# A decoder layer on eight cores: the MLP's first step ahead of the last mixer product, the last step in column halves, loads in program order

## The chip, the cores and the metric

The kernel runs on 8 cores of one Trainium2 chip. Each core does the same program on its own sequence (2048 prompt columns, 16 meta columns and 64 sample columns) with the whole set of weights; the cores don't talk to each other. The metric is the device time in microseconds of the slowest core.

## What is computed

```python
def layer(x, s_pool, s_conv, p0, ...):
    hn = rmsnorm(x, norm1_g)
    proj = hn @ w_in                                   # (B, T, 2048) = u | B | C | h
    ya, new_pool = pool_mixer(u, s_pool, p0, pool_w, pool_scale)   # causal means over 2, 4, 8, 16 rows, minus u, then 4 blocks of 128x128
    yb, new_conv = conv_mixer(bg, cg, hc, s_conv, conv_w)          # B * conv3(C * h)
    x = x + concat(ya, yb) @ w_out
    hn = rmsnorm(x, norm2_g)
    x = x + relu(hn @ w1) ** 2 @ w2                    # 1024 -> 4096 -> 1024
    return x, new_pool, new_conv
```

The layer runs once, on prompt and on sample tokens; a last rmsnorm gives y. The pooling and conv states of both are outputs too.

## The kernel before, in words

**Layout.** Features lie on the partitions, tokens in the columns. The core's 2128 columns are cut into five groups of 464, 464, 464, 448 and 288 columns (group 4 is 224 prompt and 64 sample columns). x of all groups stays in SBUF in fp32 (X1), the normed input in bf16 (H2). All else is cut from one SBUF tensor, "big", in which later buffers lie over earlier ones: w1's halves over w_in, the second w2 block over w_out, the first w2 block (W2B[0]) over UB, UBS and part of ZB, the first MLP result (A2[0]) over the rest of ZB, ZBS and PT, the second (A2[1]) and the relu tiles RB over MD and what follows.

**PSUM.** Eight banks in four pairs. Three pairs go round for all products (ps_pair), the fourth holds the two statistics banks (st_bank).

**Mixer, per group g, W(g).** A norm (Norm.whole: four squares on ScalarE, three additions of 2n columns to ACC (L520), a fold (L525), a split into a bf16 high part (L531) and a low part (L532), two ones-matmuls for the column sum (L540), Ln and Exp on ScalarE (L482, L485), eight applications (L554)). Then 32 matmuls (L626) for each of the four quarters of w_in: u, C, h, B. u is evicted to UB (u_done, L661 in groups 0 and 1, L664 later), pool_adds makes the window sums in PT (L604, L595, ScalarE's L613, L615) into MD; the last 16 columns of UB are copied to its head for the next group by GpSimd (L681). C is evicted to ZB, h multiplied in (L704), conv makes three-tap sums in CV (L718, L721, in groups 0 and 1 L727), with two columns copied to the next group's head by VectorE (L731), and b_done multiplies by B into MD (L738). There is one CV for two chunks. MD has two copies, for even and odd groups. In groups 0 and 1 the norm's factor is applied at the evictions (RSD). fold() puts pool_w into w_out (ScalarE's L786 on the pool weights, matmuls L793, evictions L796). O(g) is 64 matmuls with w_out and four adds to X (L782).

**MLP.** Twenty steps, four blocks of 1024 hidden features by five groups. w1_step is 64 matmuls, four relus on ScalarE into RB (L891) and four squares on VectorE into A2 (L894); w2_step is 64 matmuls and four adds to X (L782). In the last block each group is normed and stored as its w2_step ends (stores L587). w2_tail does the last w2_step in two halves of 144 columns, with adds L933 and the sum of squares by fp32 ones-matmuls (L548, two recorded instructions each).

**What sets the order.** Program order is written out (L860 to L875, L944 to L959):

```python
    O(0); W(2); O(1); W(3); O(2); W(4); state_out(); load_w1(0)
    O(3); O(4); load_w2(0); load_w1(1); load_w2(1); norm2(0).whole(); norm2(1).whole()
    w1_step(0)
    for si in range(ns):
        ...                       # norm2(si + 2), w1_step(si + 1), then w2_step(si) or w2_tail
```

TensorE runs its units in this order, but for the statistics matmuls, which float. All other queues are ordered by a planner (plan, L123): it simulates the program with assumed costs (VectorE 120 + 1.1 ns a column, ScalarE 150 + 0.87, GpSimd 150 + 2.2) and load times, gives each operation a due time from TensorE's schedule, and picks on each queue the ready operation that is due first; some operations may go to either of two engines. The resulting order is fixed in the program. The loads of w_in, w_out, w1, w2 and of x0 and x1 are issued by GpSimd; the other x, the pool weights (behind w_in's third quarter), the states and all stores by SyncE.

## Time and profile before

| | |
|---|---|
| time, 3 runs | 689.78 us median (689.34 to 690.92) |
| the profiled execution | 687.86 us |
| its slowest core's span (core 2) | 686.0 us |
| spans of the 8 cores | 682.2 to 686.0 us |
| mean granted TensorE clock of the cores | 0.986 to 0.992 |
| chain that ended last | PE 81%, DMA 11%, DVE 3%, issue 2% |
| read from and written to HBM | 55.69 MB, 9.24 MB |

PE is TensorE's matmuls, PEld its weight loads, DVE VectorE, ACT ScalarE, POOL GpSimd, SP SyncE. A row of the timeline has start, duration, engine, line, operation, out<-in, count and in brackets the idle time of the engine before it and what ended it. A row of a stretch has its bounds, its length, the busy time of PE, PEld, DVE, ACT and POOL, the granted clock (1.00 is full speed), the DMA share and GB/s. A row of a group has count, busy time and mean ns, idle time before it. The profile covers the slowest core; 1.9 us lie between its span and the execution's time.

### The profile page before, as it was taken

Reading aid. Unit: us, or ns where it says so; the run is one execution under the profiler, and the core shown is the slowest. Engines: PE = TensorE matmul, PEld = TensorE weight load, DVE = VectorE, ACT = ScalarE, POOL = GpSimd, SP = SyncE. Lnnn points to the kernel's source line nnn. Section 1 sums busy time; section 2 is a strip of 40 time slices with the busy share of each in tenths; the row PEclk is TensorE's granted clock in tenths of the full one; section 3 lists DMA queues with packets and bytes.
Section 4 is the critical chain, followed back from the end, with each engine's and each line's share of the span. In section 5 each row is a group of like instructions: output and inputs, shape, how many; then the busy total and the mean of one; then the engine's idle time right before and its main releaser. Section 6 shows DMA issues by size and latency. Waiting matters only on the chain.

```text
span 686.0 us, 9801 instructions; the slowest of 8 cores (682.2 to 686.0 us)
## 1 busy us (share of the span) xinstructions
PE 657.7 (96%) x3725; PEld 362.4 (53%) x3726; DVE 392.0 (57%) x542; ACT 185.7 (27%) x265; POOL 45.3 (7%) x71
## 2 busy tenths in 40 slices
PE   7969799999999999999999999999999999999993
PEld 4434354555764455565654556555556565555673
DVE  2768989789895963333333333333333333677676
ACT  3613544351615320111112101220121012433341
POOL 6411002011201000000000000000000000000000
PEclk9999999999999999999999999999999999999996
DMA  8997320000797910043340007061000000022025
GB/s 162 230 183 173 111 70 0 1 1 1 95 157 95 153 29 0 1 60 64 49 75 1 1 1 114 10 97 27 1 0 1 1 1 1 1 108 84 33 107 177
DMA packets 13598, 42.49 MB, mean 62 GB/s; under 512 B 3312, under 2 KB 7408, under 8 KB 10864
## 3 DMA queue, kind: packets, MB, share of 16 engines
q0 software_dynamic: 4672, 26.87, 23.9%
q1 hardware_dynamic: 8880, 15.00, 6.7%
q8 instruction: 30, 0.49, 0.3%
q14 instruction: 16, 0.13, 0.1%
HBM read 55.69 MB, written 9.24 MB: 95 GB/s over the span
## 4 chain that ended last, share of the span: by engine, by line
PE 81%; DMA 11%; DVE 3%; issue 2%; POOL 1%; ACT 1%; DVEq 0%; SPq 0%; ACTq 0%; POOLq 0%
PE psall L626 79%; DMA ncs<-big 5%; DMA big<-win 4%; DMA big<-pwt 2%; DVE big L554 1%; POOL big L436 1%; PE psall L548 1%; POOL big L442 1%; PE psall L540 1%; DVE big L704 1%; DVE big L520 0%; DVE big L738 0%; DVE big L721 0%; DVE big L532 0%; PE psall L793 0%
## 5 line engine op out<-in xcount | busy, mean ns | idle before, releaser
L626 PE MATMUL psall<-big 128*128 128x464 bf16 (+3 forms) x3552 | 627.7, 339 | 8.6 <-DVE big L661 5.4
L626 PEld LDWEIGHTS psall<-big 128*128 128x128 bf16 x3552 | 343.1, 98 | 291.6 <-issue 14.3
L894 DVE TENSOR_TENSOR big<-big 128x896 bf16<-128x896 f32 (+2 forms) x80 | 83.0, 1038 | 132.9 <-ACT big L891 126.7
L782 DVE TENSOR_TENSOR big<-psall,big 128x896 f32<-128x896 f32 (+2 forms) x96 | 100.5, 1048 | 100.5 <-PE psall L626 100.2
L891 ACT ACTIVATE big<-psall 128x896 f32<-128x896 f32 (+2 forms) x80 | 69.9, 874 | 289.3 <-PE psall L626 288.9
L510 ACT ACTIVATE big<-big 128x928 f32<-128x928 f32 (+3 forms) x64 | 54.9, 863 | 81.2 <-DVE big L782 37.9
L554 DVE SCALAR_TENSOR_TENSOR big<-big,psall 128x464 bf16<-128x464 f32 (+5 forms) x112 | 62.5, 611 | 4.8 <-ACT psall L485 4.7
L520 DVE TENSOR_TENSOR big<-big 128x928 f32<-128x928 f32 (+2 forms) x39 | 41.0, 1050 | 12.9 <-ACT big L510 12.6
L721 DVE SCALAR_TENSOR_TENSOR big<-big 128x448 f32<-128x448 f32 (+3 forms) x48 | 26.6, 602 | 1.6 <-ACT big L718 1.5
L604 DVE TENSOR_TENSOR big<-big 128x448 f32<-128x448 f32 (+24 forms) x47 | 25.6, 545 | 2.1 <-ACT big L664 0.9
L718 ACT ACTIVATE big<-big 128x448 f32<-128x448 f32 (+3 forms) x24 | 13.1, 582 | 29.6 <-DVE big L738 12.8
L548 PE MATMUL psall<-big 128*128 128x144 f32 (+1 forms) x48 | 14.0, 442 | 5.3 <-DVE big L554 3.6
L664 ACT COPY big<-psall 128x928 f32<-128x928 f32 (+3 forms) x16 | 10.1, 660 | 27.8 <-PE psall L626 27.7
L803 POOL DMA_DIRECT2D big<-w x8 | 4.4, 546 | 163.5 <-PE psall L626 163.5
L681 POOL COPY big<-big 128x16 f32<-128x16 f32 x16 | 10.7, 670 | 62.7 <-ACT big L613 41.8
L613 ACT ACTIVATE big<-big 128x448 f32<-128x448 f32 (+3 forms) x18 | 8.9, 494 | 20.1 <-DVE big L604 20.0
L548 PEld LDWEIGHTS psall<-big 128*128 128x128 f32 x48 | 8.7, 235 | 9.1 <-issue 8.9
L661 DVE TENSOR_TENSOR big<-psall,big 128x928 f32<-128x928 f32 x8 | 8.9, 1120 | 6.4 <-PE psall L626 6.4
L482 ACT ACTIVATE big<-psall 128x464 f32<-128x464 f32 (+3 forms) x16 | 8.0, 498 | 14.8 <-PE psall L540 11.1
L531 ACT CAST big<-big 128x464 bf16<-128x464 f32 (+2 forms) x13 | 7.1, 546 | 16.8 <-POOL big L525 9.1
L615 DVE TENSOR_TENSOR big<-big 128x448 bf16<-128x448 f32 (+3 forms) x13 | 6.7, 513 | 8.2 <-ACT big L613 8.2
L704 DVE TENSOR_TENSOR big<-psall,big 128x928 f32<-128x928 f32 (+2 forms) x10 | 10.1, 1014 | 2.0 <-PE psall L626 1.8
(40 smaller groups left out, 126.4 us busy)
## 6 DMA issues: line engine op xcount, KB each, us to landing
big<-w POOLq DMA_DIRECT2D x16, 1024.0 KB, 14.6
big<-x POOLq DMA_DIRECT2D x8, 464.0 KB, 13.1
y<-big SPq DMA_DIRECT2D x8, 464.0 KB, 2.5
y<-big SPq DMA_DIRECT2D x8, 448.0 KB, 2.7
big<-win POOLq DMA_DIRECT2D x6, 512.0 KB, 27.1
big<-wout POOLq DMA_DIRECT2D x2, 1024.0 KB, 46.5
big<-x SPq DMA_DIRECT2D x1, 1856.0 KB, 17.4
big<-x SPq DMA_DIRECT2D x1, 1792.0 KB, 8.6
```

What stands on the lines that cost most here:

```text
L510: fns = {"scalar": lambda e: e.activation(out=dst, in_=src, func=AF.Square), "vector": mul, "gpsimd": mul}
L520: P.add(self.adders, lambda e: e.tensor_tensor(out=ACC[:, :, 0:n], in0=ACC[:, :, 0:n], in1=SQ[si][:, :, 0:n], op=ALU.add), reads=[("ACC",) ...
L548: P.add("tensor", lambda e, i=i, t=t: e.matmul(out=PSP[3][:, b, 0:n], lhsT=ONES32, rhs=t, start=first and i == 0, stop=last and i == len(s ...
L554: P.add(eng, lambda e: e.scalar_tensor_tensor(out=self.dst(k, k + 1), in0=self.src(k, k + 1), scalar=self.gcol[:, k:k + 1], in1=PSP[3][:, ...
L604: P.add(("vector", "gpsimd"), lambda e, dstb=dstb, cur_src=cur_src, a0=lo, step=step: e.tensor_tensor(out=dstb[:, a0:L], in0=cur_src[:, a0 ...
L626: P.add("tensor", lambda e, k=k, i=i: e.matmul(out=PSP[b][:, t, 0:n], lhsT=lhs(k), rhs=rhs(k), start=(i == 0), stop=(i == len(ks) - 1)), r ...
L704: P.add("vector", lambda e: e.tensor_tensor(out=z, in0=PSP[b][:, :, 0:n], in1=y, op=ALU.mult), reads=pk(b) + ky, writes=zkeys(g, p), w=2 * ...
L718: P.add("scalar", lambda e, z=z, cv=cv, zo=zo, n=n: e.activation(out=cv, in_=z[:, zo:zo + n], func=AF.Copy, scale=cw[:, 0, c:c + 1]), read ...
L721: P.add(CONV_ENG, lambda e, z=z, cv=cv, a=zo + j * s, n=n, j=j: e.scalar_tensor_tensor(out=cv, in0=z[:, a:a + n], scalar=cw[:, j, c:c + 1] ...
L782: P.add("vector", lambda e: e.tensor_tensor(out=x, in0=PSP[b][:, :, 0:n], in1=x, op=ALU.add), reads=pk(b) + ks, writes=ks, w=2 * n, psum=True)
L891: P.add("scalar", lambda e, bk=bk, ri=ri: e.activation(out=RB[ri][:, :, 0:n], in_=PSP[bk][:, :, 0:n], func=AF.Relu), reads=pk(bk), writes= ...
L894: P.add("vector", lambda e, ri=ri, p=p: e.tensor_tensor(out=A2[ai][:, 2 * p:2 * p + 2, 0:n], in0=RB[ri][:, :, 0:n], in1=RB[ri][:, :, 0:n], ...
```

## The change

The planner: GpSimd's loads are issued in program order (so x0's and x1's pieces, which stand ahead in the program, are not passed by w_in's). An operation on GpSimd that uses the shared SBUF port waits in the plan for VectorE's more urgent ones. A floating statistic is placed by the time of all its operands.

```diff
+        loads = self.queued.get("gpsimd", [])
+        for op, then in zip(loads, loads[1:]):
+            op.order = then
+            then.need += 1
...
-            return port["gpsimd" if q == "vector" else "vector"]
+            if q == "vector":
+                return port["gpsimd"]
+            urgent = [o for o in pools["vector"] if o.port and o.due < op.due and o is not op and o.ready <= max(op.ready, free[q])]
+            return max(port["vector"], free["vector"] + sum(o.cost for o in urgent) if urgent else 0.0)
...
-                    if all(o.need == 0 or o.deps[-1].unit == f for o in us) and us[0].need == 0:
-                        at = max(free["tensor"], us[0].ready + lag)
+                    outer = [d for o in us for d in o.deps if not (d.eng == "tensor" and d.unit == f)]
+                    if all(d.done is not None for d in outer):
+                        at = max([free["tensor"]] + [d.done + (0.0 if d.eng == "tensor" else LATENCY["tensor"]) + lag for d in outer])
```

The buffers: group 1's u goes to U1; the second pair of conv chunks has a CV of its own (over UBS, so the pool state is loaded only in W(4)); the last group has a CV of four chunks; RB lies over MD[1] and A2[1] over MD[0]. The copies to the next group's head go to ScalarE. The square sums of whole norms may be added by VectorE or GpSimd, and the MLP's squares may be made by VectorE or ScalarE.

```diff
+    CVL = carve(4 * M_OUT[NG - 1] * 4, F32, "p (t n) -> p t n", t=4, at=CV_OFF)
+    CV2 = carve(2 * NB * 4, F32, "p (t n) -> p t n", t=2, at=UBS_OFF)
...
-    CT = carve(4 * NB * 4, F32, "p (c n) -> p c n", c=4, at=X_OFF[3])
+    CT = carve(4 * NB * 4, F32, "p (c n) -> p c n", c=4, at=H2_OFF[2])
+    U1 = carve(4 * (16 + PROMPT_COLS[1]) * 4, F32, "p (c n) -> p c n", c=4, at=X_OFF[3])
...
-    A2_OFF = [R2 + 16384, MD_OFF + 8 * NB * 2]
+    A2_OFF = [R2 + 16384, MD_OFF]
...
-    RB = [carve(2 * NB * 4, F32, "p (t n) -> p t n", t=2, at=MD_OFF + i * 2 * NB * 4) for i in range(2)]
+    RB = [carve(2 * NB * 4, F32, "p (t n) -> p t n", t=2, at=MD_OFF + 8 * NB * 2 + i * 2 * NB * 4) for i in range(2)]
...
-            self.adders = ("vector",)
+            self.adders = ("vector", "gpsimd")
...
+    def ubuf(g):
+        return (U1, "U1") if g == 1 else (UB, "UB")
...
-                P.add("gpsimd", lambda e, c=c: e.tensor_copy(out=UB[:, c, 0:H], in_=UB[:, c, L - H:L]),
-                      reads=[("UB", c, "new")], writes=[halo("UB", c)], w=60)
+        if g + 1 < NG and kn == ku:
+            P.add("scalar", lambda e: e.copy(out=un[:, c0:c0 + 2, 0:H], in_=u[:, c0:c0 + 2, L - H:L]),
+                  reads=[(ku, c, "new") for c in (c0, c0 + 1)], writes=[halo(kn, c) for c in (c0, c0 + 1)], w=60)
...
-            P.add("vector", lambda e: e.tensor_copy(out=ZB[:, c, H - 2:H], in_=ZB[:, c, L - 2:L]),
+            P.add("scalar", lambda e: e.copy(out=ZB[:, c, H - 2:H], in_=ZB[:, c, L - 2:L]),
```

The order, and the end:

```diff
-    O(0)
-    W(2)
-    O(1)
-    W(3)
...
+    for act in ("O0", "O1", "W2", "W3", "O2", "W4", "O3", "N0", "A0", "O4", "N1", "A1"):
...
+            if n == NG - 1:
+                state_out()
+                load_w1(0)
+                load_w2(0)
+                load_w1(1)
...
+    load_w2(1)
+    for si in range(ns - 2):
...
+        w2_step(si)
+        if 2 <= si + 2 < ns - 1:
+            w1_step(si + 2)
...
+    w2_step(ns - 2)
+    for half in range(2):
+        tail_w1(half)
+    for half in range(2):
+        tail_w2(half)
```

A0 and A1 are w1_step(0) and w1_step(1), N0 and N1 the second norms of groups 0 and 1. tail_w1(half) is the last w1_step on 144 of the 288 columns. tail_w2(half) is the last w2_step on them, with two PSUM pairs in turn (the "pt" counter), and the sum of squares first added up over the pairs 0 to 2 and then taken by four fp32 ones-matmuls instead of eight, into a bank of the third product pair that belongs to this half:

```diff
+            if p == 0:
+                f.square(p, acc[:, :, 0:m], ("TACC",))
+            else:
+                f.square(p, SQ[p % 2][:, :, 0:m], ("SQ", p % 2))
+            if p in (1, 2):
+                P.add(("vector", "gpsimd"), ... acc += SQ[p % 2] ...)
+        kst = ("ps", 2, half)
+        for i, (t, kt) in enumerate(((acc, ("TACC",)), (SQ[1], ("SQ", 1)))):
+            P.new_unit(True)
+            for h in range(2):
+                P.add("tensor", lambda e, ...: e.matmul(out=PSP[2][:, half, 0:m], lhsT=ONES32, rhs=t[:, h, 0:m], start=i + h == 0, stop=i + h == 2),
```

## Rows read from the trace of the kernel before

**Rows 1.** The page: busy time of the engines (us, share, instructions)

```profile
PE 657.7 (96%) x3725; PEld 362.4 (53%) x3726; DVE 392.0 (57%) x542; ACT 185.7 (27%) x265; POOL 45.3 (7%) x71
```

**Rows 2.** Busy time of each engine in three stretches; PEclk is the granted clock

```profile
0.00:80.00 80.00, 64.89 (x333) 32.61 (x335) 52.08 (x84) 31.77 (x47) 23.27 (x35) 0.98 0.84 184
180.00:240.00 60.00, 58.59 (x344) 33.24 (x342) 50.49 (x85) 22.16 (x36) 5.19 (x10) 1.00 0.93 132
...
670.00:686.00 16.00, 4.98 (x27) 4.37 (x24) 9.19 (x25) 1.47 (x4) 0.00 (x0) 0.61 0.55 189
```

**Rows 3.** TensorE in order of time, 12 to 80 us: start, duration, what, [idle before]

```profile
16.21 0.55 PE L626 MATMUL psall<-big 128*128 128x464 bf16 x2 [1.79 <-ACT big L561]
...
30.52 2.31 PE L626 MATMUL psall<-big 128*128 128x464 bf16 x11 [0.64 <-DVE big L525]
...
37.16 3.29 PE L626 MATMUL psall<-big 128*128 128x464 bf16 x16 [2.96 <-DVE big L661]
42.87 21.88 PE L626 MATMUL psall<-big 128*128 128x464 bf16 x112 [2.41 <-DVE big L661]
...
71.76 0.81 PE L793 MATMUL psall<-big 128*128 128x512 bf16 x3 [3.47 <-DVE big L731]
```

**Rows 4.** The stretch behind the last of these waits; 0.50 is the granted clock

```profile
73.00:76.00 3.00, 3.00 (x8) 1.08 (x9) 2.90 (x6) 3.00 (x5) 0.00 (x0) 0.50 0.73 225
```

**Rows 5.** The other engines in order of time, 24 to 54 us

```profile
26.58 4.45 POOL L681 COPY big<-big 128x16 f32<-128x16 f32 x2
...
40.57 2.16 DVE L661 TENSOR_TENSOR big<-psall,big 128x928 f32<-128x928 f32 x2 [0.52 <-PE psall L626]
...
51.45 1.28 ACT L786 ACTIVATE big<-big 128x128 bf16<-128x128 f32 x4 [7.20 <-DMA big<-pwt]
...
53.31 0.64 DVE L615 TENSOR_TENSOR big<-big 128x464 bf16<-128x464 f32 x1 [5.23 <-ACT big L613]
```

**Rows 6.** The DMA view: issues, KB each, median us from issue to landing

```profile
big<-pwt SPq DMA_DIRECT2D x1, 256.0 KB, 13.1
big<-sc SPq DMA_DIRECT2D x1, 64.0 KB, 2.3
ncs<-big SPq DMA_DIRECT2D x1, 64.0 KB, 31.4
```

**Rows 7.** TensorE and the GpSimd queue in order of time, 170 to 240 us

```profile
230.52 0.35 PE L540 MATMUL psall<-big 128*128 128x448 bf16 x1 [0.80 <-DVE big L532]
...
186.37 0.57 POOL L803 DMA_DIRECT2D big<-w  x1 [1.06 <-PE psall L626]
...
214.54 2.22 POOL L809 DMA_DIRECT2D big<-w  x4 [18.48 <-DMA ncp<-big]
```

**Rows 8.** The end in order of time, 660 to 686 us

```profile
669.16 4.81 DVE L554 SCALAR_TENSOR_TENSOR big<-big,psall 128x448 f32<-128x448 f32 x8
...
673.89 0.82 DVE L933 TENSOR_TENSOR big<-psall,big 128x288 f32<-128x288 f32 x2
...
674.23 4.30 PE L548 MATMUL psall<-big 128*128 128x144 f32 x16 [3.55 <-DVE big L554]
...
675.68 0.44 ACT L510 ACTIVATE big<-big 128x288 f32<-128x288 f32 x1 [5.72 <-PE psall L548]
...
679.41 2.29 DVE L554 SCALAR_TENSOR_TENSOR big<-big,psall 128x144 f32<-128x144 f32 x8 [2.50 <-ACT psall L485]
```

**Rows 9.** Matmuls of 640 to 686 us by shape: busy us, mean ns

```profile
L626 PE MATMUL psall<-big 128*128 128x144 bf16 x128 | 8.7, 226 | 0.0
L626 PE MATMUL psall<-big 128*128 128x288 bf16 x54 | 6.9, 286 | 0.0
```

**Rows 10.** The page and the groups of instructions over the whole span

```profile
L520 DVE TENSOR_TENSOR big<-big 128x928 f32<-128x928 f32 (+2 forms) x39 | 41.0, 1050 | 12.9 <-ACT big L510 12.6
...
L540 PE MATMUL psall<-big 128*128 128x464 bf16 (+2 forms) x26 | 7.3, 345 | 1.7 <-DVE big L532 1.6
...
L615 POOL TENSOR_TENSOR big<-big 128x448 bf16<-128x448 f32 (+2 forms) x5 | 6.2, 1238 | 14.9 <-DVE big L560 11.9 <-ACT big L613 2.2 <-DVE big L721 0.8
```

More of the change, by code:

```diff
@@ L50, in __init__ @@
         self.dma_counts = {}
+        self.queued = {}
         self.unit = 0
@@ L120, in dma @@
         op.dma_sem = sem; op.dma_cnt = self.dma_counts[sem]
+        self.queued.setdefault(queue, []).append(op)
         return op
@@ L180, in finish @@
             streams[op.eng].append(op)
+            if op.order is not None:
+                op.order.need -= 1
+                if op.order.need == 0:
+                    pools[op.order.eng].append(op.order)
             for s in op.succ:
@@ L478, in st_bank, with rstd @@
         return nxt("st", 2)
-    def rstd(bank, n, outs):
-        P.add("scalar", lambda e: e.activation(out=RS[:, 0:n], in_=PSP[3][:, bank, 0:n], func=AF.Ln, bias=EPS),
-              reads=[("st", bank)], writes=[("RS",)], w=n)
+    def rstd(src, ksrc, n, outs):
+        P.add("scalar", lambda e: e.activation(out=RS[:, 0:n], in_=src, func=AF.Ln, bias=EPS),
+              reads=[ksrc], writes=[("RS",)], w=n)
         for dst, key, pw in outs:
@@ L569, in whole @@
             for k in range(8):
-                self.app(k)
+                self.app(k, after)
     def norm1(g):
@@ L663, in evict @@
         else:
-            P.add("scalar", lambda e: e.copy(out=dst, in_=PSP[b][:, :, lo:hi]), reads=pk(b), writes=wr, w=2 * (hi - lo))
+            P.add("scalar", lambda e: e.copy(out=dst, in_=PSP[b][:, :, lo:hi]), reads=pk(b), writes=wr, after=after, w=2 * (hi - lo))
+    def ubuf(g):
+        return (U1, "U1") if g == 1 else (UB, "UB")
     def u_done(g, p, b):
@@ L840, in build_nc, with load_states @@
     conv_b(1)
-    load_x(3, [("WOUT", 7)], P.keys_of("CT"))
+    load_x(3, [("WOUT", 7)], P.keys_of("U1"))
     load_x(4, [("WOUT", 7)], P.keys_of("RSD"))
+    def load_states():
+        ex = [("CV", 1, t, 0) for t in range(2)]
+        P.dma("sync", lambda e: e.dma_start(out=UBS[:, :, 0:240], in_=sp_d), writes=[("UBS", c, "halo") for c in range(4)],
+              after=ex, sem="sp", nbytes=491520)
+        P.dma("sync", lambda e: e.dma_start(out=ZBS[:, :, 0:32], in_=sc_d), writes=[("ZBS", c, "halo") for c in range(4)], sem="sc", nbytes=65536)
     def W(g):
-        norm1(g).whole()
+        if g == NG - 1:
+            load_states()
+        norm1(g).whole(P.keys_of("CT") if g == 2 else ())
         W_u(g)
```

197 lines of the change are left out of this document (110 added, 87 removed).

## The prediction, made before the changed kernel was run

> **What bounds the kernel now.** The first view is the busy time of the engines [rows 1]. TensorE is busy 657.7 of 686.0 us and VectorE 392.0: nothing that shortens VectorE's work alone can pay, and the whole prize is the 28.3 us in which TensorE has nothing to do, with a few microseconds of slow clock. The second view cuts the span into stretches [rows 2]. Up to 80 us TensorE is idle 80 - 64.89 = 15.1 us, from 180 to 240 us 1.4, behind 670 us 16 - 4.98 = 11.0. That is 27.5 of the 28.3; between 80 and 640 us, but for that one spot, the kernel is solid matmul and the change, which alters neither the number nor the width of those matmuls, can gain nothing there. So three places are read closely.
>
> **The start.** TensorE's own timeline [rows 3] shows waits of 1.79 us (at 16.21), 0.64, 2.96, 2.41 and 3.47 us. The one of 2.41 us, at 42.87, comes from a chain of buffers: a matmul pair waits for its PSUM bank, that bank holds group 1's pool input, and its eviction (L661) runs only at 40.57 [rows 5], because its target UB is still read by group 0's pool sums and by halo copies on GpSimd, two of which take 4.45 us for 16 columns [rows 5]. The one of 3.47 us, at 71.76, is of another kind: VectorE is behind. ScalarE stood until 51.45 for the pool weights, a 256 KB load that took 13.1 us [rows 6], and VectorE lost 5.23 us behind that [rows 5]; from 53.31 to the wait's end it has hardly a gap. After that wait the granted clock is 0.50, TensorE's 1.2 GHz level, from 73 to 76 us [rows 4]: 3 us that do 1.5 us of work.
>
> **The change at the start.** (a) The load queue keeps program order. Before, the fourth x piece was queued behind the first w_in piece; now it is ahead. The first matmul unit needs both, so only the 1.79 us wait can shrink while the unit starts later by about one piece: about 1.5 us for the evictions, but TensorE then meets the next w_in pieces. At 30.52 it waited 0.64 us, and the add named there had ended before and is no operand, so I read this as a load. I book 0. Ends: 0 and 1.8.
> (b) Group 1 gets its own buffer U1 and the halo copies go to ScalarE. The eviction then waits only for the group's statistic, which lets the other eviction run at 34 to 36 us. The pair at 37.16 can start 1 to 2 us earlier; the one at 42.87 follows it without the gap: 2.41 + 2 = 4.4 us by there.
> (c) Second conv buffer, and 16 two-column copies off VectorE (0.15 each, about 1 us in this stretch). Against the 3.47 us wait these help only as far as VectorE's queue is shorter. The plan writes ScalarE's order from an assumed load time of 2.2 us + 262144/150 ns = 3.9 us for the pool weights against the measured 13.1, and the change leaves that alone, so ScalarE will again stand until 51.4 with conv work behind it. Behind that point, by the kernel's own count of work for group 0 and h of group 1: eight conv steps of 0.65, two products and two evictions of 1.1, four 0.6 us multiplies, some 3 us of pool sums left, 15 us: the fold starts at about 66 instead of 71.76. That is 5.8 us, and 1.5 us less the part of the clock loss that remains: 6.5. Lowest: VectorE is the bound entirely (71.76 - 53.31 = 18.4 us, of which 1 us of copies and 1 us of evictions move away): 2. Highest: all waits from 37.16 on (8.8) and the clock (1.5), less about 0.8 for the statistic: 9.5. I take 6.5.
> (d) O0 and O1 follow each other, W(2) after: the same matmuls, with 12 us more cover for norm 1 of group 2. 0; if that cover fails TensorE stands for H2, which no row of before shows.
>
> **The change in the middle.** The first MLP step (A0) goes ahead of group 4's output product. Its squares overwrite the area of ZB and ZBS, so they wait for the state stores. In the trace the 64 KB store ncs needs 31.4 us where the load of the same size, sc, with the queue empty, needs 2.3 [rows 6]: it sat beside four w1 loads, the last issued at 186.37, and the next loads waited for ncp until 214.54 [rows 7]. With A0 8 us earlier (64 matmuls of 288 columns at 0.128 [rows 9]) such a store would stop it. But the loads now keep program order, w1(0), w2(0), w1(1), and w2(0) itself waits for these stores: only two w1 loads compete, so the stores come free near 192 (the four loads ran from 174 to some 5 us before 214.54, 9 us each) and land near 197, and A0's first square is due near 202. Cost 0, hidden by O3's 12 us; the cover is 5 us wide, plus three PSUM pairs and two RB tiles. On the GpSimd queue w2(0) stands in front of w1(1) and of any pool sum planned there; w1(1) is needed five steps later. The wait of 0.80 at 230.52 [rows 7] and its like, 1.4 us [rows 2], mostly go: 1.2. Ends: -3 (a new wait like the 3.47 one) and 1.4.
> The Trainium skill (DMA: Bandwidth & Descriptors, Queues, rings and completion order) says that a DMA engine takes the queues in turn, a packet of each: a store of many small packets then crawls beside large loads. By that rule the trace agrees (31.4 against 2.3 us), and with two loads ahead in place of four the stores are late half as long.
>
> **The change at the end.** Now TensorE's last bf16 matmul ends at 674.23 - 3.55 = 670.68. VectorE is then in eight applications of group 3's final norm (669.16, 4.81 us) and reaches the last two adds at 673.89; sixteen fp32 instructions follow, at the half clock, in 4.30 us; the last eight applications start at 679.41 and the span ends 6.6 us later [rows 8]. With both halves' w1 (8 us of TensorE) behind group 3's last product, that norm is done by then. New path: hand-over 0.2, add 0.41, square 0.44 [rows 8] with 0.25 of hand-overs, two fp32 matmuls (4 instructions, 1.08 at half clock, 0.54 at full), 0.88 for the two table functions (679.41 - 678.53): first application at 673.4 to 673.9 in place of 679.41. 5.8 us. Matmuls: 64 of 288 columns become 128 of 144, 64 x (2 x 0.068 - 0.128) = 0.5 us more [rows 9]; of the 16 fp32 instructions ahead of 670.68 some 12 remain, 4 x 0.13 = 0.5 less. The adds for that sum go to VectorE or GpSimd, 0.45 each. Last, the plan's rule for floating statistics now looks at the time of every operand, where it looked at the first alone: of the 1.6 us that L540's matmuls waited for the second (L532) [rows 10], 0.8 is counted above and 0.8, at 647 and 667 us, goes here. Ends 0 and 0.8. Sum 5.8 + 0.8. Lowest for the 5.8: 2: from group 3's last product VectorE has two norms' rest and 3.6 (squares) + 3.6 (adds) + 9.3 (norm) + 1.8, some 18 us plus leftovers in 17. Highest 6.6.
>
> **Sum.** 6.5 + 1.2 + 5.8 + 0.8 = 14.3 us. Against the profiled execution's 687.86: 673.6. The median of the runs shown is 689.78, 1.9 above it: 675.5.
>
> **The rivals.**
> Rival 1, the start opens fully: the pool weights' hold does not bite, gain at the start 9.5, total 17.3: 672.5. For it: VectorE is idle 5 us before 53.31. Against it: nothing changes that load.
> Rival 2, VectorE stays the bound at the start: gain there 2, total 9.8: 680.0. For it: 18 us of VectorE without a gap.
> Rival 3, VectorE is late at the end: gain there 2, total 10.5: 679.3.
> Rival 4, the other side: additions on GpSimd. The norms' square sums may now be planned on GpSimd, at 150 + 2.2 x 928 = 2.2 us; GpSimd's five additions of up to 464 columns (L615) took 1.24 on the mean [rows 10] against 0.64 for one on VectorE [rows 5], so 928 columns are 2.5, and by my estimate up to 4 where VectorE is busy too, against 1.05 for such an add on VectorE [rows 10]. TensorE's stream is fixed, and each of 13 statistics (26 instructions [rows 10]) stops it when late; three such adds in a row are late by 1 to 5 us against the plan. It decides from 14.3/13 = 1.1 us per statistic; at 1.25 us the sum is 14.3 - 16.3 = -2.0: 691.8. Against it: the plan has a 2 us margin, and now gives GpSimd nothing while VectorE has urgent work.
> The Trainium skill (SBUF — State Buffer, Who interferes with whom) says that a VectorE instruction with two SBUF inputs and a GpSimd one that reads SBUF exclude each other for their whole length; the 4.45 us for two small copies agree.
> Rival 5, nothing: the plan reorders so that the same waits come back: within 1.4 us of 689.8.
>
> **How the numbers follow.** Forecast 0.45, rival 1 0.15, rival 2 0.17, rival 3 0.13, rival 4 0.07, rival 5 0.03. The low end 671.5 takes in rival 1 and all high terms (9.5 + 1.4 + 6.6 + 0.8 = 18.3). The upper end takes in rivals 2 and 3 and part of their sum (2 + 0 + 4 = 6, say): 684. Beyond it rivals 4 and 5 and the worst of the terms. A measurement of this kernel tells 0.2%, 1.4 us. Faster by more 0.90, within 0.03, slower 0.07.
>
> **What would show it.** Start: the L661 pairs no longer at 40.57 but by 37, no wait near 42, the fold's first matmul at 66 (rival 1: 63, rival 2: 69.5 or later), and ScalarE still standing until about 51. Middle: ncs lands in about 14 us, no TensorE wait above 0.5 between 180 and 240. End: one fp32 group at clock 1.00 and the last application 7 us before the end at most. Wrong: GpSimd busy far above 45 us with TensorE waits at L540 (rival 4), or TensorE idle for H2 after O1.

## The result, and the profile after

The changed kernel takes 677.3 us (median of 4 runs, 676.78 to 677.61) against 689.56 (4 runs, 688.41 to 690.92): a ratio of 0.9821, 95% interval 0.9801 to 0.9840, so 12.3 us faster where 14.3 were forecast. Its profiled execution took 676.78 us, 11.1 less than that of before, with spans of 673.2 to 675.2 us over the cores; core 0 is the slowest and, where no core is named, the one that is shown. Here and below, executions in which the cores of one half of the chip ran at a lower clock and over 1% longer than the others are left out of times and ratios, unless it is said otherwise.

The busy times of the page:

```profile
PE 654.8 (97%) x3774; PEld 361.9 (54%) x3774; DVE 308.3 (46%) x441; ACT 258.5 (38%) x370; POOL 58.0 (9%) x71
```

VectorE's busy time fell by 84 us, ScalarE's rose by 73 and GpSimd's by 13; TensorE's fell by 2.9 (half the fp32 statistics of the end are gone). As [rows 1] led one to expect, the 84 us of VectorE don't show in the time: TensorE is busy 97% of it.

To see where the time went, the span is cut by two marks that both kernels have: GpSimd's first w1 load, which waits for the end of group 4's u product, and the end of the last bf16 matmul. Columns as in [rows 2]. The kernel before:

```profile
0.00:174.22 174.22, 159.11 (x835) 81.72 (x837) 135.74 (x214) 69.43 (x104) 33.98 (x51) 0.99 0.41 92
174.22:670.68 496.46, 494.25 (x2876) 276.83 (x2873) 247.72 (x306) 114.82 (x159) 11.37 (x21) 1.00 0.27 47
670.68:686.00 15.32, 4.30 (x16) 3.88 (x16) 8.51 (x24) 1.47 (x4) 0.00 (x0) 0.60 0.57 198
```

The changed kernel:

```profile
0.00:172.18 172.18, 161.30 (x838) 83.15 (x839) 138.51 (x201) 77.16 (x132) 41.38 (x46) 0.98 0.41 93
172.18:664.63 492.45, 492.26 (x2930) 277.71 (x2928) 162.75 (x220) 180.24 (x237) 16.66 (x25) 1.00 0.26 49
664.63:675.20 10.57, 1.22 (x8) 1.03 (x8) 7.00 (x21) 1.13 (x4) 0.00 (x0) 0.79 0.69 199
```

The start gave 2.0 us, the middle 4.0, the end 4.75, of 10.8. By the medians over the eight cores the start gave 3.0 us (mark 173.78 before, 170.82 after) and the end 3.7. In the middle TensorE's idle time went from 2.21 to 0.19 us, eight recorded fp32 instructions are gone (four matmuls, 1.1 us), and one statistic (0.7) now stands ahead of the mark.

**The start.** TensorE in order of time:

```profile
18.31 6.43 PE L645 MATMUL psall<-big 128*128 128x464 bf16 x32
...
31.84 2.90 PE L645 MATMUL psall<-big 128*128 128x464 bf16 x14 [0.76 <-DVE big L680]
...
38.47 30.12 PE L645 MATMUL psall<-big 128*128 128x464 bf16 x144 [2.94 <-DVE big L680]
70.29 1.62 PE L829 MATMUL psall<-big 128*128 128x512 bf16 x6 [1.70 <-DVE big L774]
72.13 0.59 PE L829 MATMUL psall<-big 128*128 128x512 bf16 x2 [0.22 <-ACT big L832]
```

The wait near 42 [rows 3] is gone, but the fold begins at 70.29 (median of the cores 68.9; 71.5 before), not at 66, and the first unit at 18.31 (median 17.0; 13.6 before). The late first unit is no loss by itself: before, it stood in its midst for x (0.45 to 1.79 us over the cores), and the second unit starts at 23.3 in both kernels (medians). ScalarE, where the pool weights are converted:

```profile
53.30 1.28 ACT L822 ACTIVATE big<-big 128x128 bf16<-128x128 f32 x4 [5.91 <-DMA big<-pwt]
```

So it stood until 53.30 (median 51.9; 51.3 before). The DMA view has the loads and stores:

```profile
nps<-big SPq DMA_DIRECT2D x1, 480.0 KB, 25.1
big<-pwt SPq DMA_DIRECT2D x1, 256.0 KB, 12.9
big<-sc SPq DMA_DIRECT2D x1, 64.0 KB, 7.2
ncs<-big SPq DMA_DIRECT2D x1, 64.0 KB, 17.1
```

The conv state sc took 2.3 us in [rows 6] and takes 7.2 now (over the cores 2.3 to 4.0 before, 5.5 to 7.2 after). It no longer waits for w_out, so it is issued at 1.51 us, beside the first x pieces, which GpSimd issues from 1.58 us on.

**The middle.** The GpSimd queue:

```profile
172.18 0.58 POOL L839 DMA_DIRECT2D big<-w  x1 [6.13 <-PE psall L645]
176.10 0.53 POOL L839 DMA_DIRECT2D big<-w  x1 [3.34 <-PE psall L645]
...
199.57 1.10 POOL L845 DMA_DIRECT2D big<-w  x2 [2.08 <-DVE big L634]
200.67 1.20 POOL L839 DMA_DIRECT2D big<-w  x2
```

Two w1 loads, then w2(0) and the other pair, in the order that was forecast. What released them on six of the eight cores, this one among them, was not the stores, though, but a pool sum of group 4 (L634), which ends 27.4 us behind the first w1 load on every core. The store ncs landed after 17.1 us, at 198.5 (14 us and 197 forecast; over the cores 13.4 to 19.4 us, before 26.3 to 31.4), and between 85 and 640 us TensorE's timeline has no wait on any core; from 180 to 240 it is busy 60.00 of 60.00 us.

**The end:**

```profile
661.65 2.98 PE L645 MATMUL psall<-big 128*128 128x144 bf16 x45
...
665.11 0.45 DVE L987 TENSOR_TENSOR big<-big 128x288 f32<-128x288 f32 x1
...
665.48 6.26 DVE L573 SCALAR_TENSOR_TENSOR big<-big,psall 128x448 f32<-128x448 f32 x19
...
665.71 1.22 PE L993 MATMUL psall<-big 128*128 128x144 f32 x8 [1.08 <-DVE big L987]
...
667.40 0.29 ACT L506 ACTIVATE psall<-big 128x144 f32<-128x144 f32 x1
```

The last statistic is ready at 667.69, 3.1 us behind the last matmul's end (2.7 to 3.2 forecast). But the second half's eight applications stand in one row of 19 with three of group 3's norm and eight of the first half. The last of them ends at 671.74, and the span 3.5 us later.

### The profile page after: what moved, and what is told of

Same layout as the page of the kernel before. It is cut to its first block, busy times and chain, and to the rows that moved or that the text cites. A ratio compares the mean times of both kernels' runs of the same rounds, so it can differ in the third digit from the quotient of the medians.

```text
span 675.2 us, 9809 instructions; the slowest of 8 cores (673.2 to 675.2 us)
## 1 busy us (share of the span) xinstructions
PE 654.8 (97%) x3774; PEld 361.9 (54%) x3774; DVE 308.3 (46%) x441; ACT 258.5 (38%) x370; POOL 58.0 (9%) x71
## 3 DMA queue, kind: packets, MB, share of 16 engines
q0 software_dynamic: 4672, 26.87, 23.3%
## 4 chain that ended last, share of the span: by engine, by line
PE 87%; DMA 6%; DVE 2%; issue 2%; POOL 1%; ACT 1%; POOLq 0%; DVEq 0%; ACTq 0%; SPq 0%
PE psall L645 86%; DMA big<-win 5%; DMA big<-pwt 2%; DVE big L573 1%; POOL big L460 1%; PE psall L558 1%; POOL big L466 1%; DVE big L731 0%; DVE big L754 0%; DVE big L762 0%; ACT big L832 0%; ACT big L751 0%; PE psall L993 0%; ACT big L822 0%; ACT big L632 0%
## 5 line engine op out<-in xcount | busy, mean ns | idle before, releaser
L912 ACT ACTIVATE big<-psall 128x896 f32<-128x896 f32 (+3 forms) x84 | 70.6, 841 | 243.0 <-PE psall L645 242.8
L919 ACT ACTIVATE big<-big 128x896 bf16<-128x896 f32 (+3 forms) x79 | 69.1, 875 | 7.3 <-DVE big L543 0.3
L538 DVE TENSOR_TENSOR big<-big 128x928 f32<-128x928 f32 (+2 forms) x31 | 32.9, 1061 | 12.8 <-ACT big L528 12.0
L623 DVE TENSOR_TENSOR big<-big 128x448 f32<-128x448 f32 (+23 forms) x43 | 25.1, 584 | 2.6 <-ACT big L683 1.0
L538 POOL TENSOR_TENSOR big<-big 128x928 f32<-128x928 f32 (+2 forms) x8 | 15.9, 1989 | 39.5 <-DVE big L538 34.2
L839 POOL DMA_DIRECT2D big<-w x8 | 4.3, 536 | 171.5 <-PE psall L645 171.4
L623 POOL TENSOR_TENSOR big<-big 128x472 f32<-128x472 f32 (+8 forms) x11 | 10.6, 963 | 67.1 <-DVE big L623 55.0
L683 ACT COPY big<-psall 128x928 f32<-128x928 f32 (+3 forms) x16 | 10.1, 659 | 15.7 <-PE psall L645 15.7
L632 ACT ACTIVATE big<-big 128x448 f32<-128x448 f32 (+3 forms) x18 | 8.8, 491 | 12.6 <-DVE big L623 10.4
L918 DVE TENSOR_TENSOR big<-big 128x896 bf16<-128x896 f32 (+2 forms) x5 | 4.9, 977 | 16.4 <-ACT big L912 16.4
L567 PE MATMUL psall<-big 128*128 128x464 f32 x16 | 8.4, 679 | 3.3 <-ACT big L528 3.3
L845 POOL DMA_DIRECT2D big<-w x8 | 4.3, 537 | 79.1 <-PE psall L645 77.0
## 6 DMA issues: line engine op xcount, KB each, us to landing
big<-x POOLq DMA_DIRECT2D x8, 464.0 KB, 13.4
```

Source lines behind the costliest of these rows:

```text
L538: P.add(self.adders, lambda e: e.tensor_tensor(out=ACC[:, :, 0:n], in0=ACC[:, :, 0:n], in1=SQ[si][:, :, 0:n], op=ALU.add), reads=[("ACC",) ...
L623: P.add(("vector", "gpsimd"), lambda e, dstb=dstb, cur_src=cur_src, a0=lo, step=step: e.tensor_tensor(out=dstb[:, a0:L], in0=cur_src[:, a0 ...
L683: P.add("scalar", lambda e: e.copy(out=dst, in_=PSP[b][:, :, lo:hi]), reads=pk(b), writes=wr, after=after, w=2 * (hi - lo))
L912: P.add("scalar", lambda e: e.activation(out=RB[ri][:, :, 0:n], in_=PSP[bk][:, :, 0:n], func=AF.Relu), reads=pk(bk), writes=[("RB", ri)], ...
L919: act = lambda e: e.activation(out=out, in_=RB[ri][:, :, 0:n], func=AF.Square)
```

## The experiments

All start from the changed kernel. Times are medians in us with lowest and highest; the ratio is to the kernel before on the same chip. The changed kernel itself ran on the chip of the first runs and on B only. The kernel before has a middle core of 687.2 us on A, 683.2 on B and 684.5 on C (cores 0 to 3), so where a core's time on A or C is set against the changed kernel's, the difference holds that of two chips, and no run says how large it is. "Core" is the middle core's span (the median of the eight, then of the executions); "mark" is the issue of the first w1 load, median of the cores of the profiled execution. On chip C cores 4 to 7 ran at a granted clock of 0.97 to 0.98 in every kernel, so there both columns are of cores 0 to 3 and the times are read from them.

| kernel | chip | time | ratio, 95% | core | mark |
|---|---|---|---|---|---|
| changed, first runs | | 677.30 (676.78-677.61) | 0.9821 (0.9801-0.9840) | 674.4 | 170.8 |
| after_again | B | 676.46 (676.27-677.70) | 0.9820 (0.9802-0.9839) | 674.3 | 170.6 |
| sc_gated | A | 677.21 (676.95-677.90) | 0.9771 (0.9749-0.9793) | 674.8 | 170.7 |
| x_mixed | A | 678.77 (677.86-682.38) | 0.9800 (0.9770-0.9831) | 675.7 | 171.5 |
| pwt_at_win0 | A | 677.36 (675.26-677.99) | 0.9767 (0.9737-0.9796) | 673.5 | 169.0 |
| sc_pwt_at_win0 | A | 676.58 (674.32-681.57) | 0.9771 (0.9737-0.9805) | 672.2 | 168.4 |
| u1_shared | B | 678.36 (677.40-678.52) | 0.9841 (0.9822-0.9859) | 674.8 | 170.4 |
| cv_shared | B | 678.24 (677.44-678.53) | 0.9840 (0.9822-0.9858) | 675.3 | 172.5 |
| w_free | B | 685.65 (684.63-687.13) | 0.9950 (0.9933-0.9967) | 677.4 | |
| mid_old | C | 688.22 (687.41-688.61) | 0.9912 (0.9880-0.9943) | 679.8 | |
| tail_w1_first | C | 686.15 (685.72-687.93) | 0.9892 (0.9852-0.9933) | 677.6 | |
| tail_stat8 | C | 683.11 (682.66-683.39) | 0.9843 (0.9804-0.9882) | 674.5 | |
| both_loads | C | 683.17 (681.78-780.54), all 8 | none | 671.4 | 168.2 |

### The changed kernel again

> The changed kernel as it is, for the three runs beside it: 677.3 on the chip of the first measurement. On the chip of the four runs before, the kernel before took 693.6, and the variants 676.6 to 678.9, so here 677 to 679.

It repeats: nine executions have a middle core of 674.1 to 674.8. The kernel before on chip B has 683.2 by the same measure, 8.9 us more, but its slowest core is 4.4 us above the middle one (687.6), that of the changed kernel 0.6 (674.9; 0.4 to 1.8 over its nine executions). So of the 12.7 us that the slowest core's span lost on this chip (13.0 by the time) 8.9 are gained by the middle core, and nearly 4 are a narrower spread of the cores.

### Why the start gave 2 to 3 us instead of 6.5

Chip A, two edits of the loads (sc_gated; x_mixed issues GpSimd's first 20 loads in the planner's order as before):

```diff
-        P.dma("sync", ... in_=sc_d), writes=[("ZBS", c, "halo") for c in range(4)], sem="sc", ...
+        P.dma("sync", ... in_=sc_d), reads=[("WOUT", 7)], writes=[("ZBS", c, "halo") for c in range(4)], sem="sc", ...
```

> The changed kernel with one wait put back: the 64 KB load of the conv state (sc) again waits for the last piece of w_out, as before the change. No instruction of the four compute engines or of GpSimd moves. In the changed kernel this load has no wait and goes out at 1.5 us, among the first x pieces, and the w_in pieces land 1 to 2 us later than before. My theory, a step that the prediction left out: its 512 packets of 128 bytes delay the start. Expected: x's and w_in's pieces land 1 to 1.5 us earlier, the first product of w_in starts near 16.5 in place of 18.31 us, and the time falls by 1 to 1.5 us, to 676. Rival: the pieces come late because x now goes ahead of w_in: then nothing changes (677.3).

```diff
-        loads = self.queued.get("gpsimd", [])
+        loads = self.queued.get("gpsimd", [])[20:]
```

> The changed kernel in which only the w1 and w2 loads keep program order, so the first loads go out as before: three x pieces, the first w_in piece, the fourth x piece. The conv state still goes out first. The prediction booked 0 for this order (0 to 1.8 us gain for x first). Expected by it: within 0.5 us of 677.3. Rival: x ahead of w_in is what delays the start, then 1 to 1.5 us faster, 676.

SyncE's queue in sc_gated, core 0, and TensorE's first unit there:

```profile
64.27 0.69 SPq L884 DMA_DIRECT2D big<-sc  x1
```

```profile
15.94 3.29 PE L645 MATMUL psall<-big 128*128 128x464 bf16 x16 [0.15 <-issue]
```

The first unit starts at 15.94 (median of the cores 15.7; the changed kernel 17.0 and 16.7 in its two profiles): the early 64 KB did hold the large loads up, by 1.0 to 1.3 us. But the mark stands at 170.7, where the changed kernel has it, and the middle core at 674.8; its ratio is lower than the changed kernel's (0.977 against 0.982), but the kernel before, by which it is taken, has slower cores on chip A, and a gain at the end is neither shown nor ruled out. In x_mixed the first unit starts at 15.7 too, but it then stands 0.3 to 1.5 us for x on every core, and the second starts at 25.0 (changed kernel 23.3 and 23.0, sc_gated 22.1; medians). Its mark is 0.7 to 0.9 us later than the changed kernel's and its middle core 0.9 us later than sc_gated's. So x ahead of w_in did not cost the start its gain; by these medians it is worth 1.6 to 1.9 us at the second unit and under 1 at the mark. In both, on every core, the fold starts 17.0 to 17.2 us after the pool weights' conversion starts, as it does in the changed kernel (53.30 to 70.29 above); in the kernel before it was 20.1 to 20.3. The fold hangs on the landing of the pool weights, and what is won ahead of it is lost there.

That says what to try next: issue that load earlier and leave the plan as it is (pwt_at_win0), and with the sc gate (sc_pwt_at_win0):

```diff
         streams = self.plan()
+        late = [o for o in self.ops if o.dma_sem == "pwf"][0]
+        late.deps = [o for o in self.ops if o.dma_sem == "win0_3"]
```

> The changed kernel with the pool weights' load waiting for w_in's first quarter (about 21 us) in place of its third (about 40 us); all queues keep their order. It tests the term of the start that decided between the forecast and its first rival: ScalarE stands until 53.3 us for this load, and VectorE lost 3.67 us behind it. Theory: the weights land near 34 us, ScalarE no longer stands, the wait of 1.7 us at 70.29 goes and the fold comes at 67 to 68.5 us: 1.7 to 3 us faster, 674.3 to 675.6. Rival: VectorE's queue is the bound anyway and the early load only delays w_in's pieces by its 256 KB: 0 to 1 us slower.

> Both waits changed at once, the conv state behind w_out and the pool weights behind w_in's first quarter. If the two are separate faults of the start the gains add up: 3 to 4 us, 673.3 to 674.3. If the start is bound by what w_in's pieces allow, the second gives nothing on top of the first: 676.

pwt_at_win0, core 0 (its line numbers are 2 higher), TensorE and then ScalarE's conversion:

```profile
37.55 29.83 PE L647 MATMUL psall<-big 128*128 128x464 bf16 x144 [2.94 <-DVE big L682]
...
68.86 1.02 PE L831 MATMUL psall<-big 128*128 128x512 bf16 x4 [0.62 <-DVE big L733]
```

```profile
46.38 1.26 ACT L824 ACTIVATE big<-big 128x128 bf16<-128x128 f32 x4
```

The conversion starts at 46.38 without a wait, TensorE runs from 37.55 into the fold, and the distance is 20.8 us: the fold isn't pinned to the load any more but follows TensorE's own stream. The mark comes 1.7 us earlier (0.5 more with the sc gate), the middle core 1.3 and 2.6 us earlier than sc_gated's on the same chip. Now the sc gate pays, but 2.6 us is less than the 3 to 4 expected of the two together. By the time itself the four kernels of chip A can't be told apart (676.58 to 678.77, with overlapping intervals), since the slowest of eight cores sets it: in sc_pwt_at_win0 two executions of six have one core at 677.2 and 680.0 among others near 672.

Last, whether the two new buffers carry the start (chip B). u1_shared gives group 1's u back to UB; cv_shared has one CV for groups 0 to 3, with the sp load gated, since it fills the area that CV2 had:

```diff
-        return (U1, "U1") if g == 1 else (UB, "UB")
+        return (UB, "UB")
```

> The changed kernel without U1: group 1's pool input goes to UB again, as before the change; the rest, the copies on ScalarE too, stays. The prediction gave U1 4.4 us at the pair at 42.87. In the changed kernel every core's fold starts 17.0 us after ScalarE's hold for the pool weights ends (20.1 before the change), whatever happened ahead of it. Theory by the prediction: the 2.4 us wait near 42 is back and the time rises by 2.4 to 4.4. Rival by the traces: the wait is back, but it lies ahead of the hold, so only 0 to 1.5 us of it is seen at the end.

```diff
-        return CVL[:, 2 * p:2 * p + 2, :] if g == NG - 1 else (CV, CV2)[p]
+        return CVL[:, 2 * p:2 * p + 2, :] if g == NG - 1 else CV
...
-            kcv = ("CV", p, t, i)
+            kcv = ("CV", p if g == NG - 1 else 0, t, i)
```

> The changed kernel with one conv buffer for both pairs of chunks again in groups 0 to 3 (the last group keeps its four). The prediction gave the second buffer no price of its own. If the 3.1 us by which the distance from the hold to the fold shrank (20.1 to 17.0) are this buffer's, the fold comes 2 to 3 us later and the time rises by 2 to 3. If they are the pool sums that U1 let through earlier, nothing changes here (within 0.5) and u1_shared shows them.

u1_shared, core 2, its slowest: TensorE, and the granted clock (next to last but two) from 72 to 76 us:

```profile
37.10 26.70 PE L645 MATMUL psall<-big 128*128 128x464 bf16 x128 [2.41 <-DVE big L680]
...
70.54 1.02 PE L829 MATMUL psall<-big 128*128 128x512 bf16 x4 [1.70 <-DVE big L774]
72.22 1.86 PE L829 MATMUL psall<-big 128*128 128x512 bf16 x4 [0.66 <-ACT big L832]
```

```profile
72.00:76.00 4.00, 3.78 (x12) 1.51 (x13) 2.98 (x6) 3.82 (x6) 0.00 (x0) 0.59 0.02 4
```

The wait near 42 did not come back: on six cores there is none, and on cores 3 and 5 one of 0.77 us. The pair at 37.10 waits 2.41 us (2.94 in the changed kernel), and the mark stands where it was: U1, to which with the copies the forecast gave 4.4 us, moves no mark, and the middle core's span by 0.5 us. Something that stayed took the wait near 42 away; of this the halo copies' move from GpSimd to ScalarE stood in that chain [rows 5], but it was not undone alone. The 1.9 us in the time are not explained by that: in the profiled execution the two slowest cores, 2 and 7, are the two whose granted clock falls behind the fold; the other executions have no trace. cv_shared, core 5:

```profile
72.12 3.53 PE L829 MATMUL psall<-big 128*128 128x512 bf16 x8 [3.25 <-DVE big L774]
```

Here the fold waits 3.25 us for VectorE; over the cores 2.3 to 3.6. It starts 18.3 us after the conversion (median), between the 17.0 of the changed kernel and the 20.1 of before, so that the buffer accounts for 1.3 of these 3.1 us; the mark comes 1.9 us later, two thirds of the start's 3.0, and the middle core 1.0 us later. The 2 to 3 us that were expected did not come in full.

### Why the middle gave all that was hoped

w_free (chip B) takes the program order from the later loads, and w1(1) goes ahead of w2(0) again; mid_old (chip C) puts the first MLP step behind group 4's output product, as before:

```diff
-        loads = self.queued.get("gpsimd", [])
+        loads = self.queued.get("gpsimd", [])[:20]
```

> The changed kernel in which program order holds for the first 20 loads only: both halves of the second w1 block go out ahead of the first w2 block again, as before the change, while A0 stays ahead of O4. This tests the middle of the prediction. Theory: the conv state's store ncs crawls beside four big loads and lands near 210 to 214 in place of 198.5; A0's squares wait for it, TensorE fills three PSUM pairs, works on into O4 until about 211 and then stands 2 to 5 us: 679.5 to 682. Rival: the buffers are enough and nothing changes (within 0.5).

```diff
-    for act in ("O0", "O1", "W2", "W3", "O2", "W4", "O3", "N0", "A0", "O4", "N1", "A1"):
+    for act in ("O0", "O1", "W2", "W3", "O2", "W4", "O3", "O4", "N0", "N1", "A0", "A1"):
```

> The changed kernel with the middle in the order of before: O3, O4, both norms, A0, A1. The loads keep program order (w1(0), w2(0), w1(1)). The prediction gave the middle 1.2 us, and booked the new place of A0 itself at nothing. If what removed the waits there is the order of the loads and the statistics rule, and not A0's place, this takes no longer: 676 to 677. If A0 ahead of O4 is what covers group 4's pool sums, a wait at O4 shows and the time rises by 0.5 to 1.5.

w_free, core 1 (span 685.6), TensorE and the GpSimd queue:

```profile
204.97 4.96 PE L645 MATMUL psall<-big 128*128 128x448 bf16 x31
219.34 15.70 PE L645 MATMUL psall<-big 128*128 128x288 bf16 x90 [9.41 <-ACT big L912]
```

```profile
183.92 0.53 POOL L839 DMA_DIRECT2D big<-w  x1 [3.39 <-PE psall L645]
...
216.18 1.10 POOL L845 DMA_DIRECT2D big<-w  x2 [19.25 <-DMA ncp<-big]
```

Four w1 loads out by 183.92, ncs lands after 36.3 us, and A0's first squares, which overwrite the stored state, hold TensorE for 9.41 us. Core by core the wait follows the landing: ncs in 30.6, 32.8, 33.6, 36.3 us, waits of 3.73, 5.92, 6.72, 9.41; in 26.2 to 26.6 us, none of this kind, and spans of 674. On all five cores that wait, the wait equals the time by which ncs lands later than 36.0 us after the mark. In the changed kernel it lands 22.7 to 28.7 us after the mark; if TensorE's limit is the same there, it has over 7 us of cover. So the early A0 without the order of the loads would lose 9.2 of the 13.0 us gained on this chip, twice what I had expected.

One thing stands beside ncs that the forecast left out: nps, a store of 480 KB, is issued 8.2 to 8.4 us ahead of it on the same queue, and ncs lands 0.3 to 3.2 us behind nps on every core of the kernel before, the changed kernel and w_free. So ncs's long time is that of the stores together beside the large loads, and no run tells how it would land without nps. The Trainium skill (DMA: Bandwidth & Descriptors, Queues, rings and completion order) says that a DMA engine serves the queues in turn, a packet of each; by that rule a second large load in the other queue changes nothing for the stores while both are there, only how long they are there. The trace agrees as far as it goes: ncs takes 13.4 to 19.4 us beside two loads (changed kernel) and 26.2 to 36.3 beside four; it can't tell what this rule does to ncs from what its place behind nps does.

mid_old, core 0, TensorE and its clock behind that wait:

```profile
198.67 5.87 PE L645 MATMUL psall<-big 128*128 128x288 bf16 x33 [3.48 <-DVE big L634]
```

```profile
200.00:202.00 2.00, 2.00 (x11) 1.25 (x9) 1.17 (x2) 0.68 (x1) 0.68 (x2) 0.50 0.55 41
202.00:204.00 2.00, 2.00 (x12) 1.37 (x11) 0.09 (x1) 0.00 (x0) 0.00 (x0) 0.65 1.06 217
```

O4 waits 3.48 us for group 4's pool sums, on every core, and core 0 then loses 1.7 us to the clock (its 33 matmuls take 5.87 us, core 1's 4.20). The middle cores stand at 679.8 instead of the changed kernel's 674.3 to 674.4 on other chips. A0's place, which the forecast had only asked what it might cost, is worth about 5 us (3.48 and up to 1.7 in this trace itself) against the same kernel with O4 ahead, where 0.5 to 1.5 were expected. The kernel before, in that order, has no such wait, and the traces show why. Its last pool sum of group 4 (core 2, mark 174.22), and that of mid_old (core 0, mark 170.86):

```profile
196.99 0.22 DVE L615 TENSOR_TENSOR big<-big 128x64 bf16<-128x64 f32 x1
```

```profile
198.31 0.21 DVE L634 TENSOR_TENSOR big<-big 128x64 bf16<-128x64 f32 x1
```

It ends 23.0 us after the mark on every core before, 27.7 in mid_old and 27.4 in the changed kernel. The new plan makes these sums over 4 us later, and A0's place covers that. In mid_old TensorE stops for O4 24.3 us after the mark: sums that end at 23.0, as before, would have been in time. So the 3.48 us are the repair of a delay that the change itself brings, and no gain over the kernel before. Which of the new rules delays them was not tried.

### The end

Both on chip C. tail_w1_first puts the last w1_step ahead of group 3's last product, whole; tail_stat8 takes eight fp32 matmuls for each half's sum, without adds:

```diff
+    w1_step(ns - 1)
     w2_step(ns - 2)
-    for half in range(2):
-        tail_w1(half)
```

> The changed kernel with the last w1 step whole and ahead of group 3's last product, as before; the last w2 step keeps its new halves, statistics and buffers. The prediction named the 8 us of w1 behind group 3's product as what lets its norm be done in time. Expected by it: the last bf16 matmul ends 0.5 us earlier (no split of w1), but VectorE is late as before, with group 3's applications ahead of the last adds, and the end comes 2 to 4 us later than in the changed kernel (679 to 681). Rival: with the squares on ScalarE and additions on GpSimd VectorE has room now; then within 0.5 us.

```diff
-            if p in (1, 2):
-                P.add(("vector", "gpsimd"), ... acc += SQ[p % 2] ...)
...
+            for h in range(2):
+                P.add("tensor", lambda e, ...: e.matmul(out=PSP[2][:, half, 0:m], lhsT=ONES32, rhs=SQ[p % 2][:, h, 0:m], start=p + h == 0, stop=p + h == 4),
```

> The changed kernel with the sum of squares of each half taken by eight fp32 matmuls again, one pair of columns after the other, in place of additions and four matmuls. The changed kernel waits 1.08 us behind the last bf16 matmul for the last addition and then needs 1.22 us for four fp32 matmuls. Here 16 more recorded fp32 instructions of 0.17 us stand in TensorE's stream, 1.4 us for the 8 program matmuls more, but only two are left behind the last square. Expected: the last bf16 matmul ends about 1 us later, the chain behind it is 1 us shorter, time within 0.7 us of the changed kernel. If the additions are what the change gains by, 1 to 2 us slower.

tail_w1_first, core 1 (span 678.1):

```profile
655.22 2.16 PE L645 MATMUL psall<-big 128*128 128x144 bf16 x32 [1.34 <-DVE big L818]
...
657.88 2.72 PE L645 MATMUL psall<-big 128*128 128x144 bf16 x41 [0.50 <-DVE big L980]
...
666.30 7.44 DVE L573 SCALAR_TENSOR_TENSOR big<-big,psall 128x448 f32<-128x448 f32 x21
...
666.53 1.22 PE L993 MATMUL psall<-big 128*128 128x144 f32 x8 [1.07 <-DVE big L987]
```

Two waits of 1.34 and 0.50 us for VectorE, and 21 applications behind the last add instead of 19; from the last bf16 matmul to the span's end it is 12.5 us (cores 0 to 3) instead of 11.1. By the middle core that is 3.2 us. The w1 halves between group 3's product and the last product are the cover that the forecast named. tail_stat8, core 1 (span 675.5):

```profile
666.88 4.66 DVE L573 SCALAR_TENSOR_TENSOR big<-big,psall 128x144 f32<-128x144 f32 x16
...
667.64 0.73 PE L985 MATMUL psall<-big 128*128 128x144 f32 x4 [0.70 <-ACT big L528]
```

Here the last row of applications has 16 instructions and the last fp32 group waits 0.70 us in place of 1.08, and from the last bf16 matmul to the span's end it is 9.1 us instead of 11.1. But that matmul ends 2.0 us later, because more fp32 instructions stand ahead of it: 10.3 us behind the start of group 3's last statistic, not 8.3. The two cancel. The middle core is at 674.5 (673.5 to 675.7 over the executions), against 674.3 to 674.4 for the changed kernel on other chips; the sum by adds neither gave nor cost anything that these runs can tell, and they can't tell 1 us.

### Both load edits together

sc_pwt_at_win0 once more, on chip C:

> The kernel of sc_pwt_at_win0 once more, on the chip of these runs: the conv state's load waits for w_out, the pool weights' load for w_in's first quarter. There its spans were 671.7 to 674.8 against 673.9 to 676.4 with the first edit alone. In the changed kernel the fold follows the end of ScalarE's hold by 17.0 us on every core; here TensorE reaches the fold without a wait. Expected: 1 to 2.5 us faster than the changed kernel, 674 to 675.5 where that is at 676.5 to 677.3, a ratio to before of 0.979 where that is 0.982.

TensorE, core 0:

```profile
36.89 29.63 PE L647 MATMUL psall<-big 128*128 128x464 bf16 x144 [2.94 <-DVE big L682]
66.57 0.81 PE L831 MATMUL psall<-big 128*128 128x512 bf16 x3
68.00 1.02 PE L831 MATMUL psall<-big 128*128 128x512 bf16 x4 [0.62 <-DVE big L733]
```

Cores 0 to 3 have a middle of 671.4 us (670.2 to 671.7 over eight executions), the changed kernel 674.3 to 674.4 in its own runs, and on chip A this kernel had 672.2. That is 2 to 3 us per core better than the changed kernel, on other chips. The time of 674 to 675.5 that was expected did not come: cores 4 to 7 set it at 683.17. Changed kernel and this one were never run on the same chip, and by the slowest core the gain may be smaller.

## Why the prediction was right, and where it was not

- The time, 677.3, lies in the range and 1.8 us above the forecast; the sum of 14.3 us was made against the profiled execution, where 11.1 us came. The rest of the measured 12.3 is how the two executions lie among the others.
- That the total came this close is partly luck. On the profiled cores the start gave 4.5 us less than forecast, the middle 2.8 more and the end 1.85 less than its two terms; and the time holds a narrower spread of the cores, nearly 4 us on chip B, which the prediction did not have. The middle core of the profiled executions gained 9.5 us (683.95 to 674.45).
- **Start, term (b): mis-sized.** "2.41 + 2 = 4.4 us by there": the wait near 42 went, but u1_shared shows that U1 is not needed for that. The wait at 38.47 stayed at 2.94 us and was not a matter of UB. VectorE's timeline of core 0 has its parts: when TensorE stops at 35.5, VectorE evicts C of group 0 (35.63), makes a pool sum (L634, 36.68) and then evicts group 1's pool input (37.21), which TensorE waits for. In u1_shared, where the wait is 2.41, no pool sum stands between the two evictions.
- **Start, term (c): the step that failed.** "ScalarE will again stand until 51.4 ... the fold starts at about 66": the hold was right but for half a microsecond (median 51.9), the 15 us behind it were 17.0, and the fold came at 68.9. The work itself was counted rightly: on core 0 VectorE is busy 15.02 of the 15.13 us from 55.16 to the fold. But it was counted from the end of the hold (53.30 there), and VectorE starts 1.86 us later, when ScalarE has converted the pool weights (1.28 us) and done a pool step (L632, 0.57). With these 1.9 us, the 0.5 of the hold and the 0.4 dropped from 51.4 + 15, the 2.9 us between 66 and 68.9 are explained. What (b) won ahead of the hold could not reach past it, as the forecast had it. The start gave 2.0 to 3.0 us against 6.5; pwt_at_win0 opens the hold, and the mark moves.
- **Start, a cost that was missing.** The diff frees the conv state's load of its wait; I had listed U1, CV2 and the copies, and not the transfer that loses its wait for w_out in the same lines. It costs the first unit 1.0 to 1.3 us (sc_gated), hidden today by the hold.
- **Middle: right in the main.** The store lands at 198.5 against 197 and the waits are gone. The cover was thinner than thought for A0's first square and wider for TensorE: the square came at 200.19, not 202, and on cores 5 to 7 it waited 0.5 to 1.05 us for ncs, while by w_free TensorE stands only for a landing later than 36.0 us behind the mark, here 26.4. The reading of ncs's 31.4 us as that of a small store beside four loads left out nps, ahead of it in its queue. What I had as 1.2 us is 2.0 of idle time, and the fp32 instructions that I had booked at 0.5 under the end (four fewer) are eight fewer and 1.1. The price of the order of the loads was there in the text as a bound of 3 us; w_free has 9.2. That group 4's pool sums would come over 4 us later under the new plan, and A0's place would have to cover it (mid_old), was not in the prediction.
- **End: right in the chain, short at its end.** 4.75 us on the slowest core, 3.7 on the middle one, against 5.8. The statistic came as forecast; its applications queued behind 11 others in VectorE and ended 4.05 us after it, where eight alone take 8 x 0.29 = 2.3 (4.66 / 16 in tail_stat8).
- **The statistics' rule, 0.8 us:** the waits at that line are gone in the whole middle. Whether the rule did that or the new adders was not tried.
- **The rivals.** Rival 1 needed the hold not to bite, and it did bite. Rival 2 had the fold at 69.5 or later, the forecast at 66. By the median of the cores it came between, at 68.9; on core 0, the one profiled as slowest, at 70.29, which is rival 2's sign, and there VectorE has no gap behind the hold. Rival 2's sum of 9.8 is the nearest to the 10.8 of the spans (the forecast's 14.3 is a little nearer to the 12.3 of the times), but its reason, VectorE without a gap, is not the whole of it: with the load earlier the fold came without a wait. Rival 3 (VectorE late at the end) holds for 1.05 of its 3.8 us. Rival 4: GpSimd took eight additions of the norms (six of 896 and 928 columns at 2.1 to 2.2 us each, against 1.09 to 1.12 on VectorE, and two of 576) and its busy time rose to 58.0 us, yet TensorE waited for it once, 0.19 us at 660.36: the plan had placed them where there was time, and none came near the 4 us that I had allowed.

## What to carry to other kernels

A hold that a planner wrote from a guessed load time (3.9 us against 13) swallowed here what was won ahead of it; look for such a hold first, and move the load before the work. When a buffer gets a place of its own, list the transfers that lose their wait as well: here one went out at the first moment, beside the loads that matter. A step moved over a store's area needed the loads moved with it. And a planner that is given new freedom can make something else later: compare the last operation of each stage before and after, measured from a common mark.

## What the runs showed of the hardware

- A 64 KB load took 2.3 to 4.0 us on the eight cores with the queue empty and 5.5 to 7.2 beside the first loads. And it slows the large ones: the first unit came at 15.7 us without it and at 16.7 and 17.0 with it (medians of the cores).
- A 64 KB store behind a 480 KB one on the same queue took 13.4 to 19.4 us beside two 1 MB loads and 26.2 to 36.3 beside four, and landed 0.3 to 3.2 us behind the larger store each time (before, changed kernel, w_free).
- After a wait of TensorE of some 3.5 us the granted clock fell to 0.50 to 0.65 for about 4 us on core 0 of mid_old; on seven of its eight cores the 33 matmuls behind the wait took 5.6 to 7.0 us, on core 1, with the same wait and a clock of 1.00, 4.20. In u1_shared, with waits of 1.70 and 0.66 us at the fold, it fell on cores 2 and 7 and stayed at 1.00 on the other six, with 1.30 to 1.91 and 0.66 us. These two cores are the slowest of their execution.
- The spread of the cores is part of the time: 4.4 us from the middle to the slowest core before (chip B; 4.6 on chip A), 0.6 after (chip B; 1.4 in the first runs). In the kernel before, over 72 cores of nine executions, the span goes with the mean granted clock, but weakly (a correlation of -0.4); what else spreads them stays open.
